# Attention scores in a hybrid attention kernel: upper and lower parts stacked along the contraction, the mask from VectorE, the other branch loaded in thirds

## What is computed

```python
def diff_attend(q, k, v, lam, mask):
    """q (B,Tq,H,2,dk), k (B,Tk,H,2,dk), v (B,Tk,H,dv), mask (Tq,Tk) bool or None -> (B,Tq,H,dv)."""
    s = jnp.einsum('bqhmd,bkhmd->bhmqk', q, k).astype(jnp.float32) * (DA_DK ** -0.5)
    if mask is not None:
        s = jnp.where(mask, s, -jnp.inf)
    p = jax.nn.softmax(s, axis=-1)
    a = p[:, :, 0] - lam * p[:, :, 1]
    return jnp.einsum('bhqk,bkhv->bqhv', a.astype(v.dtype), v)
```

## Time and profile before

| | |
|---|---|
| median of 3 runs | 953.19 us (952.67 to 954.77) |
| profiled execution | 952.42 us, span 950.6 us |
| TensorE busy | 918.5 us, 97% |
| VectorE busy | 475.0 us, 50% |
| ScalarE busy | 356.5 us, 37% |
| GpSimd busy | 122.6 us, 13% |
| granted TensorE clock, mean of the span | 0.998 |

### The profile page before, as it was taken

One profiled execution on the slowest core, in us unless ns is written; L12 is line 12 of the kernel. 1 busy time (PEld: TensorE's weight loads), 2 busy tenths in 40 slices (PEclk: granted clock), 3 DMA queues, 4 the chain that ended last, 5 costly groups with the idle time before them and its releaser, 6 DMA issues. The chain is left out here.

```text
span 950.6 us, 16554 instructions
## 1 busy us (share of the span) xinstructions
PE 918.5 (97%) x6657; PEld 838.2 (88%) x6657; DVE 475.0 (50%) x1092; ACT 356.5 (37%) x853; POOL 122.6 (13%) x210
## 2 busy tenths in 40 slices
PE   5999999999999999999999999999998999999997
PEld 4799999999999999999889989998997989988884
DVE  5522276641216666244653464456447676991223
ACT  6554344422334443134443444335335332430011
POOL 1001132210102222000000000000001103440000
PEclk9999999999999999999999999999999999999999
DMA  8012011313110203251132201221124225651222
GB/s 274 6 45 67 23 47 47 91 46 99 45 45 24 61 23 99 68 192 30 39 137 73 74 2 52 67 74 46 46 76 129 82 77 170 178 168 45 89 89 77
DMA packets 85837, 74.14 MB, mean 78 GB/s; under 512 B 4697, under 2 KB 78082, under 8 KB 85506
## 3 DMA queue, kind: packets, MB, share of 16 engines
q1 hardware_dynamic: 85762, 73.09, 25.4%
HBM read 53.35 MB, written 19.73 MB: 77 GB/s over the span
## 5 line engine op out<-in xcount | busy, mean ns | idle before, releaser
L1370 PE MATMUL proj_bank<-x_hi,w_hi 128*128 128x352 f32 x1056 | 349.5, 331 | 0.9 <-ACT feature_stage L861 0.9
L1372 PE MATMUL proj_bank<-x_hi,w_lo 128*128 128x352 f32 x1056 | 339.7, 322 | 0.0
L1371 PE MATMUL proj_bank<-x_lo,w_hi 128*128 128x352 f32 x1056 | 339.0, 321 | 0.0
L1370 PEld LDWEIGHTS proj_bank<-x_hi,w_hi 128*128 128x128 f32 x1056 | 199.0, 188 | 3.7 <-issue 1.5
L1371 PEld LDWEIGHTS proj_bank<-x_lo,w_hi 128*128 128x128 f32 x1056 | 199.1, 188 | 0.0
L1372 PEld LDWEIGHTS proj_bank<-x_hi,w_lo 128*128 128x128 f32 x1056 | 198.4, 188 | 0.0
L614 DVE TENSOR_TENSOR w_lo<-w_raw,w_hi 128x1024 fp32r<-128x1024 f32 x49 | 59.9, 1223 | 76.1 <-ACT w_hi L610 76.1
L963 ACT ACTIVATE probs<-score_banks,softmax_stats 128x128 f32<-128x128 f32 (+8 forms) x72 | 51.2, 713 | 77.8 <-DVE softmax_stats L1286 69.0
L1031 POOL TENSOR_TENSOR stats<-stats,minus_half 128x1 f32<-128x1 f32 (+1 forms) x36 | 22.3, 620 | 371.7 <-DVE stats L1319 371.7
L1016 POOL TENSOR_TENSOR decays<-log_decay 128x128 f32<-128x128 f32 (+1 forms) x122 | 48.1, 426 | 162.6 <-ACT log_decay L908 162.6
L610 ACT ACTIVATE w_hi<-w_raw 128x1024 fp32r<-128x1024 f32 (+1 forms) x53 | 55.1, 1039 | 15.6 <-PE proj_bank L1372 14.7
(11 more groups left out here) (183 smaller groups left out, 1411.5 us busy)
## 6 DMA issues: line engine op xcount, KB each, us to landing
w_raw<-in_w_in SPq DMA_DIRECT2D x44, 512.0 KB, 4.6
merge_tanh_scratch<-feature_stage SPq DMA_DIRECT2D x16, 528.0 KB, 3.0
feature_stage<-merge_tanh_scratch SPq DMA_DIRECT2D x10, 528.0 KB, 3.7
x_rows<-in_x_prompt SPq DMA_DIRECT2D x8, 512.0 KB, 6.0
w_raw<-in_w_out SPq DMA_DIRECT2D x8, 512.0 KB, 4.5
branch_out<-in_x_prompt SPq DMA_DIRECT2D x8, 512.0 KB, 3.6
out<-branch_out SPq DMA_DIRECT2D x8, 512.0 KB, 2.6
tokens_stage<-merge_tanh_scratch SPq DMA_DIRECT2D x6, 528.0 KB, 3.7
```

The lines of the kernel that those rows point to most:

```text
L1370: nc.tensor.matmul(out, wh, xh, start=first, stop=False)
L1371: nc.tensor.matmul(out, wh, xl, start=False, stop=False)
L1372: return nc.tensor.matmul(out, wl, xh, start=False, stop=last)
```

## The change

Each map's scores become matmuls over all 128 rows. The keys are kept twice, `k_stacked` [128, 2, keys] in fp32r: for map m, its 64 rows hold the upper part (rounded) and the other 64 rows the lower part. The queries of one tile are laid out against that in `q_stacked` [128, 4, 128]: slice 2m has the upper part of q in both halves, slice 2m+1 the lower part of q against the keys' upper part and zeros against their lower part. Two matmuls per map and block of keys give hi·hi + hi·lo and lo·hi (L1660, L1661).

New stages make these: `qd` (four ScalarE copies and two VectorE subtractions for the next step's query tile, right after `aS`), `ks` (two copies and two subtractions for each third of a key tile, right after its unit) and `kc` (the same for the cached keys). Keys pass through a feature stage buffer. The constant mask matmul and its load are gone; VectorE writes -1e30 over 64 by 64 scores before each maximum of a prompt tile. The other branch is loaded in three DMAs, each once its third of the last projection unit is done, straight to where its lower part will stand.

```diff
+        if kind == "dk":
+            stages.append(("ks", i, th))
...
+            stages.append(("obload", th))
...
+        if n == 0:
+            stages.append(("qd", 0, 0))
...
         if now:
             stages.append(("aS",) + now)
+        if at_step(s + 1):
+            stages.append(("qd",) + at_step(s + 1))
...
+        if now and now[1] == 1:
+            stages.append(("kc", now[0]))
...
-        if s == NTT:
-            stages.append(("obload",))
...
-                    sp.wait_ge(s_obst, 16)
-                    sp.dma_start(t_["OBS"][:, :, :].rearrange("p h t -> p (h t)"), ob_dram).then_inc(s_obld, 16)
+                    th = st[1]
+                    cols = slice(TH * th, TH * (th + 1))
+                    if th == 0:
+                        sp.wait_ge(s_obst, 16)
+                    sp.wait_ge(s_unit, unit_no(NP_ - 1, th) + 1)
+                    sp.dma_start(BLB[:, :, cols].bitcast(F), ob_dram.rearrange("p (h t) -> p h t", h=H)[:, :, cols]).then_inc(s_obld[th], 16)
...
+            def keys_hi(h, cols, src, s_hi):
+
+                for m in range(2):
+                    r = slice(64 * m, 64 * m + 64)
+                    last = nc.scalar.activation(t_["K"][h % 2][r, m, cols], src[r, :], ACT.Copy)
+                last.then_inc(s_hi, 1)
...
-                    elif tk == "dk":
-                        nc.scalar.activation(t_["K"][i % 2][:, cols], bank, ACT.Copy).then_inc(s_uout, 1)
...
-                    act.wait_ge(s_unit, unit_no(NP_ - 1, st[1]) + 1)
-                    act.wait_ge(s_obld, 16)
-                    nc.scalar.activation(BHB[:, :, cols], t_["OBS"][:, :, cols], ACT.Copy).then_inc(s_bh, 1)
+                    act.wait_ge(s_obld[st[1]], 16)
+                    nc.scalar.activation(BHB[:, :, cols], BLB[:, :, cols].bitcast(F), ACT.Copy).then_inc(s_bh, 1)
...
+                elif kind == "qd":
+                    h, i = st[1], st[2]
+                    s, n = NTT * h + i, ntok(i)
+                    if s == 0:
+                        act.wait_ge(s_gl, 2 * NTT - 1)
+                    if s >= 2:
+                        act.wait_ge(s_sc, 2 * (s - 1))
+                    if i == 0:
+                        act.wait_ge(s_uout, units_done(ft_at["dq", h]))
+                    for m in range(2):
+                        for e in (m, 1 - m):
+                            last = nc.scalar.activation(t_["QD"][s % 2][64 * e:64 * e + 64, 2 * m, 0:n],
+                                                        t_["Q"][h % 2][64 * m:64 * m + 64, tok(i)], ACT.Copy)
+                    last.then_inc(s_qdh, 1)
+                elif kind == "ks":
+                    h, th = st[1], st[2]
+                    t, cols = ft_at["dk", h], slice(TH * th, TH * (th + 1))
+                    if h >= 2 and th == 0:
+                        act.wait_ge(s_sc, 2 * NTT * (h - 1))
+                    act.wait_ge(s_uout, unit_no(t, th) + 1)
+                    keys_hi(h, cols, FT[ft_no[t] % NFT][:, cols], s_ksh)
+                elif kind == "kc":
+                    h = st[1]
+                    freed(act, ("cache", h))
+                    keys_hi(h, slice(T, KC), t_["CK"][:, :, :].rearrange("p i f -> p (i f)"), s_kch)
...
+            def keys_lo(h, cols, src, s_done):
+
+                for m in range(2):
+                    r, other = slice(64 * m, 64 * m + 64), slice(64 - 64 * m, P - 64 * m)
+                    K = t_["K"][h % 2]
+                    last = nc.vector.tensor_tensor(K[other, m, cols], src[r, :], K[r, m, cols].bitcast(F), ALU.subtract)
+                last.then_inc(s_done, 1)
...
+                        if i < TT:
+                            w = nk - 64
+                            link(nc.vector.memset(SC[0:64, 2 * m + w // 512, w % 512:w % 512 + 64], BIG))
...
+                elif kind == "ks":
+                    h, th = st[1], st[2]
+                    cols = slice(TH * th, TH * (th + 1))
+                    dve.wait_ge(s_ksh, 3 * h + th + 1)
+                    keys_lo(h, cols, FT[ft_no[ft_at["dk", h]] % NFT][:, cols], s_ks)
+                elif kind == "qd":
+                    h, i = st[1], st[2]
+                    s, n = NTT * h + i, ntok(i)
+                    QD, Q = t_["QD"][s % 2], t_["Q"][h % 2]
+                    if s == 0:
+                        dve.wait_ge(s_gl, 2 * NTT - 1)
+                        for x in t_["QD"]:
+                            nc.vector.memset(x[64:P, 1, :].bitcast(F), 0.0)
+                            last = nc.vector.memset(x[0:64, 3, :].bitcast(F), 0.0)
+                        last.then_inc(s_qdz, 1)
+                    dve.wait_ge(s_qdh, s + 1)
+                    for m in range(2):
+                        r = slice(64 * m, 64 * m + 64)
+                        last = nc.vector.tensor_tensor(QD[r, 2 * m + 1, 0:n], Q[r, tok(i)], QD[r, 2 * m, 0:n].bitcast(F),
+                                                       ALU.subtract)
+                    last.then_inc(s_qd, 1)
+                elif kind == "kc":
+                    h = st[1]
+                    dve.wait_ge(s_kch, h + 1)
+                    keys_lo(h, slice(T, KC), t_["CK"][:, :, :].rearrange("p i f -> p (i f)"), s_kc)
...
-                        pe.wait_ge(s_mrld, 16)
-                    nb = -(-nk // 512)
-                    for b in range(nb):
-                        w = min(512, nk - 512 * b)
-                        cc = slice(c0 + 512 * b, c0 + 512 * b + w)
-                        masked = i < TT and b == nb - 1
-                        done = [None, None]
-                        for m in range(2):
-                            r = slice(64 * m, 64 * m + 64)
-                            if s and b == 0:
-                                pe.wait_ge(s_ex, 2 * s - 1 + m)
-                            done[m] = nc.tensor.matmul(SC[0:n, 2 * m + b, 0:w], t_["Q"][h % 2][r, tok(i)],
-                                                       t_["K"][h % 2][r, cc], start=True, stop=not masked)
-                        for m in range(2) if masked else ():
-                            r = slice(64 * m, 64 * m + 64)
-                            done[m] = nc.tensor.matmul(SC[0:n, 2 * m + b, w - 64:w], t_["MR"][r, 0:P],
-                                                       t_["MR"][r, P:P + 64], start=False, stop=True)
+                        pe.wait_ge(s_qdz, 1)
+                    pe.wait_ge(s_qd, s + 1)
+                    QD, K = t_["QD"][s % 2], t_["K"][h % 2]
                     for m in range(2):
-                        done[m].then_inc(s_sc, 1)
+                        if s:
+                            pe.wait_ge(s_ex, 2 * s - 1 + m)
+                        for b in range(-(-nk // 512)):
+                            w = min(512, nk - 512 * b)
+                            keys = K[:, m, c0 + 512 * b:c0 + 512 * b + w]
+                            out = SC[0:n, 2 * m + b, 0:w]
+                            nc.tensor.matmul(out, QD[:, 2 * m, 0:n], keys, start=True, stop=False)
+                            last = nc.tensor.matmul(out, QD[:, 2 * m + 1, 0:n], keys, start=False, stop=True)
+                        last.then_inc(s_sc, 1)
```

61 lines of the change are left out of this document (32 added, 29 removed).

## The result

| | before | after |
|---|---|---|
| median | 953.2 us (952.7 to 954.8) | 1041.4 us (1038.5 to 1042.9) |
| ratio, 95% interval | | 1.092 [1.091, 1.094] |
| span of the profiled execution | 950.6 us | 1036.7 us |
| TensorE busy / idle in the span | 918.5 / 32.1 us | 931.2 / 105.5 us |
| VectorE, ScalarE busy | 475.0, 356.5 us | 524.9, 417.0 us |

The change costs 88 us. The direction was forecast; the size was not: 997 was expected, and 1041 lies outside 957 to 1014. Of the 86.1 us by which the span grew, TensorE's idle time is 73.4 and its busy time 12.7, though it has less to do.

What follows compares the result with a forecast made beforehand. TensorE was taken to bound the attention stage, busy 353.2 of 358.0 us. Terms -11 + 29 + 19 + 6 + 1 = +44 us on 952.4 gave 996.4, 997 as a median, range 957 to 1014.

Steps and rivals of the forecast that it cites:

- the eleven token transposes: Attention steps with a token transpose after their first half unit; each was to be delayed 2.4 to 2.9 us.
- Rivals 1 and 2: Half the waits hidden: 969 us, chance 0.24; waits cost nothing and the 15.3 us stay: 938 us, chance 0.10.
- The load in thirds at nothing: Other branch's load: waits for thirds of the last projection, hidden by the next unit, so no cost.
- rival C: Follow-ups' rival: stacked matmuls, VectorE mask, load in thirds or side-engine load cost time wherever they stand; no overall chance given.
- 4. The clock falls: Rival: TensorE stalls up to 3.5 us drop its clock to 1.2 GHz; 20 us of such work give 1017; chance 0.04.
- Saved: 15.3 us: Attention scores on TensorE: 53.4 us become 38.1, 0.27 to 0.55 a step, from the mask and the borders.
- other 25 steps: Attention steps outside the eleven with token transposes; 11 of the 15.3 us saving was to be left there.
- 29 us together: Token transposes in eleven steps wait for VectorE's late read-out of the value product, 2.4 to 2.9 us each.
- about 0.84: Time in us of four overlapping ScalarE query copies of 64x128 after the second exponential, ahead of VectorE's subtractions.
- 19 us: Key thirds and cache keys delay VectorE's weighted sum, stalling the next transposes: 17 us, plus 2.5 in short steps.
- The rest: Gated-branch products of steps (3,4) to (3,7) wait for VectorE's read-out: could lose 10 us, 6 taken.
- The recurrence's 1: Recurrence phase: one key third stands before a read-out; 1 to 2 us, 1 taken.

Runs made afterwards that it cites:

- e1: The changed kernel with the next queries' copies and subtractions behind the first token transposes or in the middle of the first projection: 996.0 us, ratio 1.045.
- e2: The changed kernel with key halves of heads 1 to 3 and the cache in the middle of the next step's first projection: 1021.1 us, ratio 1.072.
- e9: e8 with the branch's first third loaded 300 us earlier into its own buffer and split in the projection before the last: 953.3 us, ratio 1.0003.
- e10: e5 without the two VectorE memsets that write the mask into the scores: 954.4 us, ratio 1.0016.
- e6: The changed kernel with 335 unused projection matmuls filling TensorE's stalls ahead of token and probability transposes: 1028.2 us, ratio 1.079.
- e5: The changed kernel with queries, keys and the branch's first split late, and ScalarE's copies of queries and one key third ahead of the exponentials: 962.5 us, ratio 1.0104.
- e8: e5 with two da_out buffers, its read-out ahead of da_out_normed, and the first head's key halves in the middle of the next projection: 956.2 us, ratio 1.0033.
- e11: e9 with the second map's mask copied into the scores by ScalarE instead of VectorE: 950.6 us, ratio 0.9966.

## Why the prediction was wrong

**What held.** The mechanism and its places: VectorE waits at the new subtractions for q_stacked; TensorE waits ahead of exactly the eleven token transposes named, and behind the key halves; e1 and e2 take both away by order alone. Rivals 1 and 2 (the waits half hidden, or costing nothing) are out. The load in thirds at nothing held only loosely: ScalarE stood 1.49 us for it once and VectorE's maxima of step (3,4) came later; e9 gets 3.0 us by loading the first third early. Of rival C, then, two pieces cost time in the good order too: the mask on VectorE (e10) and this load.

**The step that failed most: "4. The clock falls", given 0.04 and left out of the sum.** The text reasoned that a granted clock of 1.00 over 12 us in which TensorE was hardly busy speaks against it. That row can't show it: in the stall of step (0,3) the clock reads 1.00 too, and 0.52 only after TensorE has gone on. The price was e6's 16 us for the token and key stalls. In the whole kernel it is more: without the long stalls TensorE is busy 907 to 910 us (e5, e8, e9, e11), in the changed kernel 931.2, so **some 22 us are matmuls at the lower level**, near the 20 that the rival had taken; its 1017 misses the rest, since it stood on the forecast's waits. The Trainium skill (TensorE: Matmul & The Clock Gate, Why this matters for your kernels) warns of idle gaps between bursts of matmuls. The trace agrees with it in step (0,3), 0.52 behind a gap of 3.31 us, and not at 458.5 us, 1.00 behind one of 3.37. The 0.04 rested on the one row against the rival, and that row could not bear it.

**The saving: "Saved: 15.3 us", 11 of it left.** Busy time shows 8 to 12 (918.5 to 910.2 in e5, to 906.8 in e8). The matmuls were sized right; step (1,7) on TensorE's timeline, now in e11:

```profile
565.13 0.27 PE L1732 MATMUL turn_bank<-ident,da_out_normed 128*128 128x128 f32 x1
565.15 0.48 PE L1696 MATMUL score_banks<-k_stacked,q_stacked 128*128 128x512 f32 x1
565.47 0.39 PE L1697 MATMUL score_banks<-k_stacked,q_stacked 128*128 128x512 f32 x1
...
567.09 1.50 PE L1724 MATMUL turn_bank<-da_v,probsT 128*128 128x128 f32 x12
```

From the transpose to the value product it is 567.09 - 565.13 = 1.96 us; 1.86 for the scores, 0.02 and the transpose's own 0.11 make 1.99. Before it was 567.75 - 565.47 = 2.28. What was off is what comes of it: the product behind short scores waits for ScalarE's probsT (2.0 us in 5 places in e11, 1.1 in 2 before), and the "other 25 steps" were taken as TensorE's own, where VectorE's weighted sums hold up some (3.7 us in e11, 1.9 before).

**The token term: "29 us together"** was counted from today's end. With the 4 us that it takes as saved inside those steps it stands for 33 us of waits, and 36.6 were measured. The copies are the mis-sized link: "about 0.84" took from the earlier trace rows that small ScalarE instructions overlap; four of 64x128 took 1.25, 0.31 each, one after the other. In step (0,3) that is 1.15 us from the end of the exponential's read (439.51 to 440.66), 0.31 more than forecast, and eleven times that, 3.4 us, is about the difference. The memsets cost what was said or less (0.11 each); the subtractions 0.59 as said.

**Keys: "19 us"** measured 20.6 less the 1.9 of before, 18.7. This term was right. e2 takes 17.2 of these waits away, and gave 20.3 us with its share of the clock.

**"The rest": 6 us for the gated branch** measured 12: TensorE's waits at L1453 for an instruction issue and at L1672 for da_out are 13.4 us there, 1.4 before. The forecast priced VectorE's read-out alone; the first product also waits for ScalarE's read-out of the last projection, which stands behind two exponentials, four copies and the split. The recurrence's 1 was 2.7, and the three cache transposes (2.4 us) were not counted.

**The account.** Forecast: idle +59, busy -15. Measured: idle +73.4 (36.6 tokens, 18.7 keys, 12 branch, 2.7, 2.4, and 1 in small ones), busy +12.7 (some 10 saved, 22 of slow clock). Of the miss of 44 us, 28 is busy time (the clock and the smaller saving) and 14 is idle time (the copies, the branch, the cache); the other 2 lie between the median and the profiled execution. That the whole of the branch's 12 us comes from the order was not tried apart; e5 to e9 show that most of it goes with it.

## What to carry to other kernels

Before work is moved to a half-idle engine, look where in that engine's order it will stand: the same six instructions a step cost 45 us more ahead of a read-out than in the middle of a projection, where TensorE waits 3 us for them. Where a TensorE-bound stage has places at which VectorE ends within 0.2 us of TensorE, count both as the bound: there 0.22 us of memsets a step cost 6 to 8 us in all, and taking 0.26 us of matmuls a step away gave 2. And where new stalls of some microseconds come, allow for slow matmuls behind them; here these were some 22 us for 73 us of added idle time, though only about half of the stalls had them.

## What the runs showed of the hardware

- Where the clock falls, it falls behind a stall, not in it: 1.00 granted while TensorE stood 3.31 us, then 0.52 for 3.4 us from about 1 us after it went on, matmuls of 352 columns 0.29 us apart instead of 0.16. A shorter one did it too: the matmuls around the wait at 686.2 us start 2.47 us apart, and from 687.4 us they run at half speed. Others did not, up to one of 3.37 us at 458.5 us, with 1.00 granted until 464.
- ScalarE's fp32r copies of 64 partitions by 128 cost 305 ns each and did not overlap; with half the partitions they are hardly cheaper than the 320 ns of 128 by 128.
- Mask matmuls of 64 columns hold 0.26 us of the timeline of a step and free 0.16 when they go. Whether the 0.10 that stays is the border behind half-height matmuls was not tried apart.
